# Retention: the product of scores and values as three fp32r products instead of one fp32 product

## The reference

```python
def retention_chunk_scan(q, k, v, log_gamma, state0, with_out):   # one direction
    ...
        new_state = state * chunk_dec + einsum('bhsd,bhse->bhde', kc * k_dec, vc)
        scores = einsum('bhcd,bhsd->bhcs', qc, kc) * intra
        out = einsum('bhcs,bhse->bhce', scores, vc) + einsum('bhcd,bhde->bhce', qc * q_dec, state)

def retention_mixer(h_lat, h_ctx, w_in, w_o, ...):
    q_c, k_c, v_c, g_c = project(h_ctx, w_in)     # h @ w_in, cut into heads
    q_l, k_l, v_l, g_l = project(h_lat, w_in)     # q_l, k_l are then rotated
    ...                                           # forward and backward scans, added
    y_lat = finish(o_lf + flip(o_lb), g_l)        # normalise, * silu(g), @ w_o
    y_ctx = finish(o_cf + flip(o_cb), g_c)
```

## Time and profile before

| | before |
|---|---|
| median of three runs | 2667.2 us |
| the three runs | 2666.24, 2667.20, 2668.75 us |
| span of the profiled execution | 2664.4 us |
| PE busy | 2503.6 us, 94% of the span |
| DVE busy | 1308.2 us, 49% |
| ACT busy | 500.3 us, 19% |
| retention in the profile | about 1380 to 1835 us |

### The profile page before, as it was taken

The page is one execution under the profiler, slowest core; times in us unless marked ns, Lnnn a source line. Parts: engine busy times, 40 slices in busy tenths (PEclk is TensorE's granted clock), DMA queues, the critical chain, the costliest instruction groups (busy, mean ns, idle before and its releaser), DMA issues.

```text
span 2664.4 us, 44818 instructions
## 1 busy us (share of the span) xinstructions
PE 2503.6 (94%) x18374; PEld 1839.7 (69%) x18374; DVE 1308.2 (49%) x2733; ACT 500.3 (19%) x684; POOL 25.4 (1%) x46
## 2 busy tenths in 40 slices
PE   6998999999999999999989999998999998996998
PEld 5887665555555555555566778777888887775897
DVE  2446443333333333333364535537655456776876
ACT  1111200000000000000022223132222223332432
POOL 0000000000000000000000000000000000000000
PEclk8999999999999999999989999998999999998999
DMA  8788899999999999999941222121332222322652
GB/s 337 295 310 338 321 392 420 422 422 422 422 422 422 422 422 422 422 422 422 421 161 64 79 74 85 63 79 64 116 103 97 95 79 95 112 89 89 221 187 78
DMA packets 94077, 661.33 MB, mean 248 GB/s; under 512 B 10512, under 2 KB 11168, under 8 KB 15984
## 3 DMA queue, kind: packets, MB, share of 16 engines
q1 hardware_dynamic: 89360, 642.10, 61.0%
q0 software_dynamic: 4608, 17.66, 2.0%
HBM read 658.66 MB, written 1.05 MB: 248 GB/s over the span
## 4 chain that ended last, share of the span: by engine, by line
PE 77%; DMA 10%; DVE 8%; SPq 2%; issue 2%; ACT 1%; DVEq 0%; ACTq 0%
PE bank L190 20%; PE bank L1830 10%; PE bank L1811 9%; DMA diag_gtmp<-in_panels_e 8%; PE bank L1698 6%; PE bank L1750 3%; PE bank L1684 3%; PE bank L1290 3%; PE bank L1586 2%; PE bank L1567 2%; PE bank L1147 2%; DMA ring<-in_units_a 2%; SPq L668 2%; PE bank L1729 2%; PE bank L1907 1%
## 5 line engine op out<-in xcount | busy, mean ns | idle before, releaser
L190 PE MATMUL bank<-ring,scratch 128*64 128x256 f32 x2176 | 249.8, 382 | 0.0
L190 PEld LDWEIGHTS bank<-ring,scratch 128*64 128x64 f32 x2176 | 150.2, 137 | 94.9 <-issue 26.2
L945 ACT ACTIVATE scratch<-scratch 128x256 f32<-128x256 f32 x68 | 28.3, 416 | 804.5 <-DVE scratch L2589 804.5
L2593 DVE TENSOR_SCALAR scratch<-bank 128x256 f32<-128x256 f32 x68 | 28.9, 425 | 225.3 <-PE bank L190 225.3
L2954 DVE TENSOR_TENSOR w_lo<-ring,w_hi 128x2048 fp32r<-128x2048 f32 x46 | 105.3, 2290 | 67.5 <-ACT w_hi L1037 67.4
L2589 DVE TENSOR_SCALAR scratch<-bank 128x256 f32<-128x256 f32 x68 | 28.9, 425 | 202.1 <-PE bank L190 202.1
L1811 PE MATMUL bank<-hT_hi,w_hi 128*128 128x512 f32 (+1 forms) x352 | 126.0, 358 | 0.8 <-ACT mtmp L1048 0.8
L190 PE MATMUL bank<-hT,scratch 128*64 128x256 f32 x1088 | 125.6, 381 | 0.0
L1830 PE MATMUL bank<-w_hi,hid_hi 128*128 128x512 f32 x320 | 124.7, 390 | 0.6 <-DVE hid_lo L2962 0.6
L1811 PE MATMUL bank<-hT_hi,w_lo 128*128 128x512 f32 (+1 forms) x352 | 125.1, 355 | 0.0
L1811 PE MATMUL bank<-hT_lo,w_hi 128*128 128x512 f32 (+1 forms) x352 | 125.1, 355 | 0.0
(11 more groups left out here) (544 smaller groups left out, 5129.9 us busy)
## 6 DMA issues: line engine op xcount, KB each, us to landing
ring<-in_panels_e SPq DMA_DIRECT2D x136, 1024.0 KB, 25.6
ring<-in_units_a SPq DMA_DIRECT2D x88, 1024.0 KB, 7.0
hid<-in_panels_e SPq DMA_DIRECT2D x68, 1024.0 KB, 25.2
hT<-in_panels_e SPq DMA_DIRECT2D x68, 1024.0 KB, 25.5
ring<-in_panels_m SPq DMA_DIRECT2D x64, 1024.0 KB, 5.1
yacc<-in_panels_e SPq DMA_DIRECT2D x34, 1024.0 KB, 25.4
diag_gtmp<-in_panels_e SPq DMA_DIRECT2D x34, 1024.0 KB, 26.2
rows<-in_panels_e SPq DMA_DIRECT2D x34, 1024.0 KB, 26.1
```

The costliest lines, as they stand in the source:

```text
L190: m = self.pe.matmul(b[s * rows:(s + 1) * rows, 0:cols], lhs(k), v[:, s * cols:(s + 1) * cols], start=(first and k == 0), stop=(k == KT - 1))
```

## The change

The product in `mixed` is made of three fp32r products. Both operands get an upper and a lower part: ACT now writes the upper part of the values (`rv_hi`) and signals a new semaphore `vg_upper`; DVE subtracts it from the bank (`values_low`, four operations of 128 x 512 per head) and only then signals `vg_free`. In `scores()` DVE multiplies into a scratch tile `rtmp`, copies it to `rsT_hi` and subtracts to `rsT_lo`; after the sixth tile it signals PE (`to_tensor.send`), and PE's `mixed` waits for that signal in place of the two free banks.

```diff
         with ExitStack() as stages:
+            rv_lo = stages.enter_context(nc.sbuf_tensor("rv_lo", [P, 4, 512], F32R))
...
+            rsT_lo = stages.enter_context(nc.sbuf_tensor("rsT_lo", [P, 6, SEQ], F32R))
...
+            rv_hi = stages.enter_context(nc.sbuf_tensor("rv_hi", [P, 4, 512], F32R))
+            rsT_hi = stages.enter_context(nc.sbuf_tensor("rsT_hi", [P, 6, SEQ], F32R))
...
-            def columns_out(i, which, unit, fn):
+            def columns_out(i, which, unit, fn, out):
...
-                    fn(t, quad[t][:, :]).then_inc(vg_free, 1)
+                    fn(t, quad[t][:, :]).then_inc(out, 1)
 
             def values_out(i, unit):
-                columns_out(i, 0, unit, lambda t, b: act.copy(rv[:, t, :], b))
+                columns_out(i, 0, unit, lambda t, b: act.copy(rv_hi[:, t, :], b), vg_upper)
...
             def mixed(i):
-                S.read()
+                from_dve.get()
                 for t in range(4):
                     pe.wait_ge(vg_free, 8 * i + 4 + t + 1)
                     src = [(n, n) for n in range(4)] if t < 2 else [(4, 2), (5, 3)]
                     for n, key in src:
-                        m = pe.matmul(quad[t][:, :], rsT[:, n, (t % 2) * P:(t % 2) * P + P], rv[:, key, :],
-                                      start=(n == src[0][0]), stop=(n == src[-1][0]))
+                        for c, (x, y) in enumerate(three):
+                            m = pe.matmul(quad[t][:, :], (rsT_hi, rsT_lo)[x][:, n, (t % 2) * P:(t % 2) * P + P],
+                                          (rv_hi, rv_lo)[y][:, key, :], start=(n == src[0][0] and c == 0),
+                                          stop=(n == src[-1][0] and c == 2))
                     m.then_inc(mixed_full, 1)
...
                 for n in range(6):
                     b = S.take()
                     w = Wc[:, n - 2, :] if n in (2, 3) else Wd[:, n % 2, :]
-                    S.done(stt(rsT[:, n, :], b[:, 0:SEQ], 1.0 / 16, w, ALU.mult, ALU.mult))
+                    m = stt(rtmp[:, n % 2, :], b[:, 0:SEQ], 1.0 / 16, w, ALU.mult, ALU.mult)
+                    S.done(m)
+                    dve.wait_ge(side.free, S.c.at(2))
+                    step(copy(rsT_hi[:, n, :], rtmp[:, n % 2, :]))
+                    m = tt(rsT_lo[:, n, :], rtmp[:, n % 2, :], rsT_hi[:, n, :], ALU.subtract)
+                to_tensor.send(m)
+
+            def values_low(i, unit):
+                for t in range(4):
+                    dve.wait_ge(vg_upper, 4 * i + t + 1)
+                    tt(rv_lo[:, t, :], quad[t][:, :], rv_hi[:, t, :], ALU.subtract).then_inc(vg_free, 1)
...
             lower(4)
+            values_low(0, 3)
             spread(0)
...
                     lower(n + 6)
+                    values_low(i + 1, n + 5)
                     decays()
                     lower(n + 7)
```

More of the change, by code:

```diff
@@ L305, in program @@
         tok = sb("tok", 4, D)
+        with ExitStack() as stages:
+            rv_lo = stages.enter_context(nc.sbuf_tensor("rv_lo", [P, 4, 512], F32R))
         xn = sb("xn", XT, D)
@@ L312, in program @@
         tail = CONST_COLS - (LEVELS + 3) * P
+        with ExitStack() as stages:
+            stages.enter_context(nc.sbuf_tensor("below_s", [P, tail], F32))
+            rsT_lo = stages.enter_context(nc.sbuf_tensor("rsT_lo", [P, 6, SEQ], F32R))
         cst = sb("cst", tail + 2048)
@@ L379, in program @@
             rot_hi, rot_lo = [stages.enter_context(nc.sbuf_tensor(n, [P, 4, 512], F32R)) for n in ("rot_hi", "rot_lo")]
+        with ExitStack() as stages:
+            stages.enter_context(nc.sbuf_tensor("below_v", [P, 2 * KT * 512 + 4096 + 7680], F32))
+            rv_hi = stages.enter_context(nc.sbuf_tensor("rv_hi", [P, 4, 512], F32R))
+            rsT_hi = stages.enter_context(nc.sbuf_tensor("rsT_hi", [P, 6, SEQ], F32R))
         with ExitStack() as stages:
@@ L476, in program @@
         vg_free = sem("vg_free")
+        vg_upper = sem("vg_upper")
         mixed_full = sem("mixed_full")
@@ L610, in program @@
         We = carve(7168, 2, SEQ)
-        rv = carve(7680, 4, 512)
-        rsT = carve(9728, 6, SEQ)
         rtmp = carve(11264, 2, SEQ)
@@ L975, in columns_out @@
                         act.wait_ge(vg_full, 6 * i + 3 * which + t + 1)
-                    fn(t, quad[t][:, :]).then_inc(vg_free, 1)
+                    fn(t, quad[t][:, :]).then_inc(out, 1)
             def values_out(i, unit):
-                columns_out(i, 0, unit, lambda t, b: act.copy(rv[:, t, :], b))
+                columns_out(i, 0, unit, lambda t, b: act.copy(rv_hi[:, t, :], b), vg_upper)
             def gates_out(i, unit):
-                columns_out(i, 1, unit, lambda t, b: act.activation(rg[:, t, :], b, ACT.Silu))
+                columns_out(i, 1, unit, lambda t, b: act.activation(rg[:, t, :], b, ACT.Silu), vg_free)
             def decays(i):
```

## The result

| | before | after |
|---|---|---|
| median | 2668.3 us (6 runs, 2666.2 to 2670.5) | 2678.2 us (6 runs, 2675.2 to 2681.5) |
| profiled execution, its own time | | 2681.3 us |
| its span | 2664.4 us | 2679.5 us |
| mean granted clock of PE in it, as a share of full speed | 0.979 | 0.975 |

The ratio is 1.0037 (95% interval 1.0026 to 1.0049): 9.9 us slower, where 6.2 were forecast. Both medians lie within the stated range.

A forecast was written before the change was run, and what follows sets the result against it. PE was taken to bound retention, with two small waits on DVE chains. Terms of -8.2, +8.6, +2.4 and +3.4 us sum to +6.2, on 2667.2 giving 2673.4 us; range 2668 to 2680.

The forecast's parts named there:

- Term 1: PE's product in `mixed`: three fp32r products replace each fp32 one, -2.06 us a head, -8.2 us for four.
- Term 2: Score tiles on DVE: 1.14 us each, over PE's 0.864, so `mixed` starts 2.16 us later a head, +8.6 us.
- the lower bound: Score tiles: if their DVE chain were no longer than PE's pace, only the last copy and subtraction add, 0.79 us a head.
- Term 3: Lower parts of the values: four DVE subtractions delay head 0's gates, +2.4 us once; covered in heads 1 to 3.
- Term 4: PE's clock in retention: falls behind head 0's wait and two of four `mixed`, one old fall gone, +3.4 us.
- The waits only: Rival: DVE's chains as forecast, but the clock holds or old falls go as new come; 2670.0 us, chance 0.26.
- The clock falls at every new pause: Rival: clock falls in four heads' `mixed` and at head 0's gates, old falls kept; +11.3, 2678.5 us, chance 0.12.
- The clock comes back: Rival: old falls behind transposes and the last head's wait nearly all go, new pauses keep the clock; 2659.7 us, chance 0.04.
- a cover fails: Rival: `lower(n + 7)` or a value bank comes late in heads 1 to 3; about 2682 us, chance 0.04.

The follow-up runs named there:

- the product alone: Against the kernel before: `mixed` makes three fp32r products, all of upper parts, with no lower parts made; 2661.0 us, ratio 0.9968.
- the score parts alone: The kernel before, fp32 products kept, with DVE also making both parts of each score tile, unused, and PE waiting for the last; 2687.3 us, ratio 1.0067.

## Why the prediction was right, and where it was off

**Term 1** (-8.2 us): right. With full clock 36 products took 8.31 us, a head became 2.10 us shorter for the forecast's 2.06, and the product alone gained 8.5 us (5.3 to 11.7).

**Term 2** (+8.6): right. A tile took 1.12 us for 1.14, `mixed` started 7.93 us after the scores for 8.02, 2.07 us later than before; four times that is 8.3. The lower part of unit n + 1 and the statistics delayed nobody: no other wait appears in the list. With the copy on ScalarE, PE's pace of 0.86 us a tile came back, and 0.90 us a head was added, near the lower bound's 0.79.

**Term 3** (+2.4 in head 0, nothing elsewhere): right. The wait grew from 1.54 to 3.93, by 2.39 us, and in heads 1 to 3 no wait for the gates' second unit or for a bank appears.

The sum of these three can be read by itself. Retention less its lost clock took 419.5 and 419.2 us in the two executions of the kernel before and 422.5 in both of the change: 3.0 to 3.3 us more, for the forecast's 2.8.

**Term 4** (+3.4): the mechanism, a clock lost behind the new pauses, was right and the size was off. Head 0 fell as forecast. I took two of the four pauses of 1.9 us and it was all four, in both executions: 8.5 us of new falls for the 5.1 that I counted. I took one of the three old falls as gone, and all three were gone, but against the first profile, whose three falls are not firm: in a second execution of the kernel before there were none. Against the first, the net is +3.4, and retention +6.4 for the forecast's 6.2, which is luck: two misses cancel. Against the second it is +8.5 - 1.7 = +6.8, and retention +10.1. The measured 9.9 and 7.7 us lie between. What was mis-sized is the number of pauses that cost the clock, four and not two, and under it lies a wrong step: one execution's falls of the clock were read as a base to subtract from.

**The rivals.** "The waits only" is out, by the five windows and by the filled pauses. "The clock falls at every new pause" is what happened at the new pauses, and its 2678.5 us stand next to the first measurement's 2678.2. But it kept the old falls, which the change has in neither execution; the kernel with the score parts alone has both. I gave this rival too little. The Trainium skill, TensorE: Matmul & The Clock Gate, section "A second HAM failure mode: psum-queue depth-cycling", puts such a loss down to small pauses between groups of matmuls. The trace agrees only in that the clock was lost. With the long pause filled and the small ones between score tiles left, the clock stayed at 1.00, so the small ones alone do not cost it here; whether they add to what the long one does is not shown. "The clock comes back" and "a cover fails" did not happen.

**Left open.** Why the falls at the new pauses are firm in the change, while the pause of 1.90 us in the last head of the kernel with queries and keys ahead of `mixed` cost nothing, and why those behind the transposes come and go in one and the same kernel, was not settled.

## What to carry to other kernels

Three fp32r products cost four fifths of one fp32 product, so making the parts must be nearly free: put the pass that makes them behind work of PE that needs none of them, or on an engine that doesn't set the pace, and the same change goes from 0.3% slower to 0.3% faster. An added step in a hand-written list of an in-order engine should stand behind whatever PE is waiting for at that place. And a pause of PE can cost more than its length: in this kernel allow 1.7 us for a lost clock with each new pause of about 2 us, though not every one loses it, and compare several executions before a fall in one is taken as given.

## What the runs showed of the hardware

- Pauses of 1.90 us ahead of `mixed` cost the clock eight times of eight in the two executions of the change, at 1.7 us each, and 15 times of 17 over all kernels here that have them. Pauses of 1.41 us there never did (five cases), nor did a single pause of 1.54 us (five) or 2.36 us (three) at the gates of head 0; one of 3.93 us did in all three cases. The length alone doesn't decide it.
- The pair of pauses of 0.96 and 1.40 us around the transposes cost the clock in 15 of 36 cases: in three of three in one execution of the kernel before, in none of three in another.
- Eight matmuls of 128 x 512 in each pause ahead of `mixed` and 16 in the one at the gates kept the clock at 1.00 there, where it had lost 8.5 us in all.
- Waits and starts in the two executions of the kernel before repeat to 0.1 us; nearly all of their difference of 3.7 us in retention is granted clock (3.4).
- On DVE a follower that waits for its forerunner's result starts 0.04 us after the recorded end of it (1453.05 after 1452.59 + 0.42), and one that waits for nothing 0.09 us before it (1453.72, for 1453.38 + 0.43).
